# Sorting sample scores by merge steps, an earlier selection and a fifth slot for query slices in a fused decoder layer

## The reference, cut to what matters

```
z = rms_norm(x) @ w_in                      # u, q, k, v, iq, ik, iw
score = sum_h relu(iq_h . ik) * iw_h        # one score per query and key
keys  = top_k(score, k)                     # k = 64 of 256 (prompt), 256 of 1028 (sample)
yb    = softmax(q . k / sqrt(128)) over those keys @ v ;  ya = pooling mixer(u)
x1    = x + concat(ya, yb) @ w_o
q2    = rms_norm(x1) @ w_pq ;  s = q2 . sub_keys     # 16 slices of 128 columns
16 best pairs per head -> 128 experts per token
y     = x1 + sum_e g_e * gelu(h . expert_u[e]) * expert_v[e]
```

## Time and profile before

| what | us |
|---|---|
| three runs | 981.14, 981.31, 981.70 (median 981.31) |
| the profiled execution, its own time | 981.55 |
| its span, first to last instruction | 980.1 |
| PE busy | 958.2 (98% of the span) |
| DVE busy | 777.5 (79%) |
| ACT busy | 558.6 (57%) |
| POOL busy | 438.6 (45%) |

### The profile page before, as it was taken

One profiled execution on the slowest core, in us unless ns is written; L12 is line 12 of the kernel. 1 busy time (PEld: TensorE's weight loads), 2 busy tenths in 40 slices (PEclk: granted clock), 3 DMA queues, 4 the chain that ended last, 5 costly groups with the idle time before them and its releaser, 6 DMA issues.

```text
span 980.1 us, 19215 instructions
## 1 busy us (share of the span) xinstructions
PE 958.2 (98%) x6440; PEld 835.3 (85%) x6440; DVE 777.5 (79%) x1805; ACT 558.6 (57%) x1092; POOL 438.6 (45%) x328
## 2 busy tenths in 40 slices
PE   5999999999999999999999999999999999999998
PEld 2347879899999999999999998888888888888887
DVE  2569987269999948999999976777888878788873
ACT  2023354454445559999999975654555555555552
POOL 4643465145788776776777770011212211131200
PEclk9999999999999999999999999999999999999999
DMA  9635748668855554444445456797888888888872
GB/s 330 149 109 160 238 139 308 209 226 316 280 176 175 180 185 150 152 161 160 150 155 165 151 173 217 257 337 283 300 300 305 299 279 296 303 304 303 291 263 94
DMA packets 75424, 221.24 MB, mean 226 GB/s; under 512 B 11301, under 2 KB 23725, under 8 KB 74964
## 3 DMA queue, kind: packets, MB, share of 16 engines
q1 hardware_dynamic: 60812, 179.12, 53.7%
q0 software_dynamic: 12800, 40.36, 13.3%
q10 hardware_dynamic: 1744, 0.92, 0.4%
HBM read 217.41 MB, written 3.14 MB: 225 GB/s over the span
## 4 chain that ended last, share of the span: by engine, by line
PE 86%; DVE 4%; DMA 4%; ACTq 2%; ACT 2%; issue 2%; SPq 0%; DVEq 0%
PE psum L1123 33%; PE psum L1059 22%; PE psum L1060 12%; PE psum L1071 3%; PE psum L1055 3%; PE psum L603 3%; PE psum L872 2%; ACTq L402 1%; PE psum L873 1%; DMA w_raw<-expert_v 1%; DMA rows_in<-expert_u,eidx 1%; PE psum L581 1%; DMA w_raw<-expert_ut 1%; DVE work L1825 1%; PE psum L887 1%
## 5 line engine op out<-in xcount | busy, mean ns | idle before, releaser
L1630 POOL TENSOR_TENSOR w_lo<-w_raw,w_hi 128x1024 fp32r<-128x1024 f32 x116 | 279.1, 2410 | 124.1 <-ACT w_hi L1170 123.9
L1059 PE MATMUL psum<-h_split,w_hi 128*128 128x256 f32 x1792 | 327.0, 284 | 1.3 <-issue 1.3
L1060 PE MATMUL psum<-h_split,w_lo 128*128 128x256 f32 x1024 | 289.4, 283 | 0.0
L1059 PEld LDWEIGHTS psum<-h_split,w_hi 128*128 128x128 f32 x1792 | 279.2, 192 | 2.6 <-issue 1.4
L1170 ACT ACTIVATE w_hi<-w_raw 128x1024 fp32r<-128x1024 f32 x214 | 224.9, 1051 | 39.4 <-DMA w_raw<-expert_ut 27.6
L1060 PEld LDWEIGHTS psum<-h_split,w_lo 128*128 128x128 f32 x1024 | 196.1, 191 | 0.0
L2145 DVE TENSOR_TENSOR w_lo<-w_raw,w_hi 128x1024 fp32r<-128x1024 f32 x98 | 120.5, 1229 | 54.7 <-ACT w_hi L1170 54.4
L1123 PE MATMUL psum<-w_hi,ag_hi 128*128 128x512 f32 x512 | 158.2, 390 | 0.4 <-DVE ag_lo L2152 0.4
L1123 PE MATMUL psum<-w_hi,ag_lo 128*128 128x512 f32 x512 | 158.0, 389 | 0.0
L1170 ACT ACTIVATE ag_hi<-store 128x256 fp32r<-128x256 f32 x128 | 53.2, 417 | 152.5 <-PE psum L1123 152.4
L1123 PEld LDWEIGHTS psum<-w_hi,ag_hi 128*128 128x128 f32 x512 | 95.8, 188 | 20.6 <-ACT w_hi L1170 0.8
(11 more groups left out here) (347 smaller groups left out, 1485.0 us busy)
## 6 DMA issues: line engine op xcount, KB each, us to landing
w_raw<-expert_ut SPq DMA_DIRECT2D x128, 512.0 KB
w_raw<-expert_v SPq DMA_DIRECT2D x86, 512.0 KB
raw_more<-expert_v SPq DMA_DIRECT2D x42, 512.0 KB, 4.8
w_slice<-w_pq_cols SPq DMA_DIRECT2D x32, 512.0 KB, 5.3
w_most<-w_in_blocks SPq DMA_DIRECT2D x8, 699.0 KB, 11.3
w_slice<-w_o_half SPq DMA_DIRECT2D x8, 512.0 KB, 4.7
v_cache<-cache_v POOLq DMA_DIRECT2D x64, 64.0 KB, 3.7
w_o_sb<-w_o_half SPq DMA_DIRECT2D x8, 512.0 KB, 6.1
```

The costliest lines, as they stand in the source:

```text
L1059: pe.matmul(out, w_hi[:, s, c, :], h_split[:, c, a], start=(c == 0 and a == 0), stop=False)
L1060: mm = pe.matmul(out, w_lo[:, s, c, :], h_split[:, c, 0], start=False, stop=(c == KC - 1), skip_group_check=wide)
L1630: pool.tensor_tensor(w_lo[:, s], w_raw[:, s], w_hi[:, s].bitcast(F32), ALU.subtract).then_inc(S["w_lo_ready"], 1)
```

## The change

1. The 32 rounds become 36 merge steps (`sort`), each a maximum and a minimum of 128 x 128 elements over rows of 256, spread 11, 10, 5, 4, 4 and 2 over the same places; a step with d = 0 reads its second operand backwards. `insert` puts the 257th score in.
2. `join`, the eight `order` steps and `cut` all come ahead of `add_wo(0)`, `tally` and `admit` between `add_wo(0)` and `add_wo(3)`.
3. A fifth place `w_slice_x` (where `probT` lies later) for slices 4 and 9; SP loads slices 0, 4, 1, 2, 3 first, later ones as their place comes free (`before(r)`), and w_o_sb beside slices 7 to 14 instead of 6 to 13.
4. `low_q(1)` and `low_q(2)` move from POOL to DVE, `low_q(0)` ahead of `join_sq(4)` on POOL, and POOL's `v_cache` groups follow without a break. `high_q(2)` moves up on ACT, and `copy_q(r)` stands ahead of `high_q` where it stood behind it. `high_q(11)` now stands ahead of `rs_copy(1)`.

The diff, with context and assertions cut and the new `w_slice_x` and `q_lo_x` (both at `cur[0] - NPG * P`) left out:

```diff
@@ -331,12 +333,12 @@
...
     S = Named(nc, ctx)
-    w_slice_in = [ctx.enter_context(nc.semaphore(f"w_slice_in{i}")) for i in range(SLICES)]
+    w_slice_in = [ctx.enter_context(nc.semaphore(f"w_slice_in{i}")) for i in range(SLICES + 1)]
     row_in = [ctx.enter_context(nc.semaphore(f"row_in{i}")) for i in range(2)]
...
-    Q_FIRST = 3
+    Q_FIRST = 1
@@ -345,9 +347,28 @@
...
+    R_SLOT = (0, 1, 2, 3, 4, 0, 1, 2, 3, 4, 0, 1, 2, 3, 0, 1)
+    assert len(R_SLOT) == RSLOTS and KC == 2 * SLICES
+    def r_turn(r):
+        return (2 if R_SLOT[r] < SLICES else 0) + R_SLOT[:r + 1].count(R_SLOT[r])
+    def s_turn(i, j):
+        return 2 + R_SLOT.count(j) + i + 1
+    def before(r):
+        return max([x for x in range(r) if R_SLOT[x] == R_SLOT[r]], default=-1)
+    def q_raw(r):
+        return w_slice[:, R_SLOT[r]] if R_SLOT[r] < SLICES else w_slice_x[:]
...
-        return q_lo[:, (KC + r) % SLICES]
+        return q_lo[:, R_SLOT[r]] if R_SLOT[r] < SLICES else q_lo_x[:]
@@ -459,21 +480,30 @@
...
-            Q_PQ, Q_SAMPLE = KC, KC + RSLOTS
...
-                old = q - SLICES
-                if old >= Q_SAMPLE:
-                    sp.wait_ge(S["rq_s_psum"], (old - Q_SAMPLE) // 4 + 1)
-                elif old >= Q_PQ:
-                    sp.wait_ge(S["rq_psum"], old - Q_PQ + 1)
-                elif old >= 4:
-                    sp.wait_ge(S["wo_psum"], 2 * (old - 4) + 2)
-                elif old >= 0:
-                    sp.wait_ge(S["wo_half"], old + 1)
-                src = w_o_half[q] if q < Q_PQ else w_pq_cols[(q - Q_PQ) % RSLOTS]
-                sp.dma_start(w_slice[:, q % SLICES], src).then_inc(w_slice_in[q % SLICES], 16)
+                if q >= SLICES:
+                    sp.wait_ge(S["wo_half"], q - SLICES + 1)
+                sp.dma_start(w_slice[:, q % SLICES], w_o_half[q]).then_inc(w_slice_in[q % SLICES], 16)
+            def load_q(r):
+                if r < SLICES:
+                    sp.wait_ge(S["wo_psum"], 2 * r + 2)
+                elif before(r) < 0:
+                    sp.wait_ge(S["yb_psum"], 2)
+                else:
+                    sp.wait_ge(S["rq_psum"], before(r) + 1)
+                sp.dma_start(q_raw(r), w_pq_cols[r]).then_inc(w_slice_in[R_SLOT[r]], 16)
+            def load_sample(i):
+                for j in range(SLICES):
+                    if i:
+                        sp.wait_ge(S["rq_s_psum"], i)
+                    else:
+                        sp.wait_ge(S["rq_psum"], max(r for r in range(RSLOTS) if R_SLOT[r] == j) + 1)
+                    sp.dma_start(w_slice[:, j], w_pq_cols[SLICES * i + j]).then_inc(w_slice_in[j], 16)
@@ -491,8 +521,10 @@
...
             k_loads(32, K_SP - 32)
-            for q in range(4, 12):
+            for q in range(4, KC):
                 load_slice(q)
+            for r in (0, 4, 1, 2, 3):
+                load_q(r)
             sp.wait_ge(S["zp_copied"], 8)
@@ -505,14 +537,14 @@
...
                              ).then_inc(S["rows_out"], 16)
-            for q in range(12, 14):
-                load_slice(q)
+            for r in (5, 6):
+                load_q(r)
             sp.wait_ge(S["log_g_done"], 2)
             for i in range(8):
-                load_slice(14 + i)
+                load_q(7 + i)
                 sp.dma_start(w_o_sb[:, i].rearrange("p a k j -> p (a k) j"), w_o_half[i]).then_inc(S["w_o_in"], 16)
-            for q in range(22, Q_SAMPLE):
-                load_slice(q)
+            for r in range(15, RSLOTS):
+                load_q(r)
@@ -531,15 +563,12 @@
...
                 load_u(s, s)
-            for q in range(Q_SAMPLE, Q_SAMPLE + SLICES):
-                load_slice(q)
+            load_sample(0)
             for n in range(FRONT):
...
                 if n % 4 == 1 and n < 12:
-                    q = Q_SAMPLE + SLICES * (n // 4 + 1)
-                    for i in range(SLICES):
-                        load_slice(q + i)
+                    load_sample(n // 4 + 1)
                 if n == 8:
@@ -998,7 +1027,7 @@
...
                 for j in range(4):
-                    slice_in(KC + RSLOTS + 4 * i + j)
+                    pe.wait_ge(w_slice_in[j], 16 * s_turn(i, j))
                 if i:
@@ -1290,10 +1319,10 @@
...
-                act.wait_ge(w_slice_in[(KC + r) % SLICES], 16 * ((KC + r) // SLICES + 1))
+                act.wait_ge(w_slice_in[R_SLOT[r]], 16 * r_turn(r))
                 if 3 <= r < 13:
                     act.wait_ge(S["rq_psum"], r - 1 if r >= 11 else r - 2)
-                copy(q_high(r), w_slice[:, (KC + r) % SLICES]).then_inc(S["q_hi_ready"], 1)
+                copy(q_high(r), q_raw(r)).then_inc(S["q_hi_ready"], 1)
@@ -1301,6 +1330,7 @@
...
+            high_q(2)
             act.wait_ge(S["rstd_half"], 2)
@@ -1341,27 +1371,24 @@
...
                 copy(h_split[:, c, 0, :], h2[:, c, 0:SEQ]).then_inc(S["h_hi_p"], 1)
-            high_q(2)
             copy_log(0)
             copy_log(1)
-            for r in range(3, 7):
+            for r in range(3, 8):
+                copy_q(r - 3)
                 high_q(r)
-                copy_q(r - 3)
-            high_q(7)
-            copy_q(4)
             act.wait_ge(S["rows_out"], 16 * (9 + 1 + DB))
             rs_copy(act, copy, 0)
+            copy_q(5)
             high_q(8)
-            copy_q(5)
             sample_exp(0)
+            copy_q(6)
             high_q(9)
-            copy_q(6)
+            copy_q(7)
             high_q(10)
-            copy_q(7)
             sample_exp(1)
             copy_q(8)
+            high_q(11)
             rs_copy(act, copy, 1)
-            high_q(11)
             copy_q(9)
@@ -1618,12 +1645,9 @@
...
             join_sq(2)
+            low_q(0)
             join_sq(4)
-            low_q(0)
-            low_q(1)
-            v_loads(V_FIRST + 4, 4)
-            low_q(2)
-            v_loads(V_FIRST + 8, DB * NPG - V_FIRST - 8)
+            v_loads(V_FIRST + 4, DB * NPG - V_FIRST - 4)
@@ -1814,16 +1838,26 @@
...
-            def rounds(n):
-                for _ in range(n):
-                    r = done[0]
-                    left = score4[:, :] if r == 0 else work4[:, :]
-                    best = sorted4[:, 8 * r:8 * r + 8]
-                    settle(dve.max(best, left))
-                    if r < ROUNDS - 1:
-                        settle(dve.match_replace(work4[:, :], best, left, TAKEN))
+            lists = (sorted4, work4)
+            HALVES = [(1 << m, d) for m in range(STAGES) for d in [0] + [1 << e for e in range(m - 1, -1, -1)]]
+            def sort(n):
+                for half, d in HALVES[done[0]:done[0] + n]:
+                    old = score4 if done[0] == 0 else lists[(done[0] + 1) % 2]
+                    a, b = (x[:, 0:QK].rearrange("p (n h k) -> p n h k", h=2, k=d or half)
+                            for x in (old, lists[done[0] % 2]))
+                    one, two = a[:, :, 0], a[:, :, 1] if d or half == 1 else a[:, :, 1, ::-1]
+                    dve.tensor_tensor(b[:, :, 0], one, two, ALU.max)
+                    settle(dve.tensor_tensor(b[:, :, 1], one, two, ALU.min))
                     done[0] += 1
+            def insert(_):
+                new = score4[:, QK:QW]
+                dve.tensor_tensor(sorted4[:, 0:1], work4[:, 0:1], new, ALU.max)
+                settle(dve.scalar_tensor_tensor(sorted4[:, 1:QK], work4[:, 0:QK - 1], new, work4[:, 1:QK],
+                                                ALU.min, ALU.max))
@@ -1880,31 +1914,39 @@
...
+            def low_q(r):
+                dve.wait_ge(S["q_hi_ready"], r + 1)
+                dve.tensor_tensor(q_low(r), q_raw(r), q_high(r).bitcast(F32), ALU.subtract
+                                  ).then_inc(S["q_lo_dve"], 1)
             done = [0]
-            STAGES = 8
-            assert QK == 1 << STAGES and ROUNDS * 8 == KSEL_S == QK
-            rounds(6)
+            assert QK == 1 << STAGES and KSEL_S == QK and len(HALVES) % 2 == 0
+            sort(11)
             rope_qk(2)
-            rounds(5)
+            sort(10)
             select_p(0)
-            rounds(3)
+            sort(5)
             select_p(1)
             norm_p(0)
-            rounds(2)
+            sort(4)
             max_p(1)
-            rounds(2)
+            sort(4)
             norm_p(1)
-            rounds(ROUNDS - done[0])
+            sort(len(HALVES) - done[0])
+            insert(0)
+            join(0)
+            for stage in range(STAGES):
+                order(stage)
+            cut(0)
             add_wo(0)
-            join(0)
-            for i in range(1, 5):
+            tally(0)
+            add_wo(1)
+            add_wo(2)
+            admit(0)
+            for i in range(3, KC):
                 add_wo(i)
-                order(2 * i - 2)
-                order(2 * i - 1)
-            add_wo(5)
-            cut(0)
-            add_wo(6)
-            add_wo(7)
+            low_q(1)
             norm2_p(0)
@@ -1912,16 +1954,7 @@
...
-            def low_q(r):
```

(14 more changed lines are left out.)

## The result

Median 984.62 us over 18 runs (981.28 to 987.14) against 981.17 for the kernel before on the same chip (18 runs, 979.04 to 983.36): ratio 1.0037, 95% interval 1.0027 to 1.0047, which is 2.6 to 4.6 us **slower**. Run again beside other kernels, the changed kernel gave 1.0025 (1.0007 to 1.0043). The forecast was 981.8, with 978.8 to 984.0 as its range: the median is just outside it, and a slowdown was held to be less likely (0.24) than no change (0.57). One run of the kernel before, among those beside d1 to d4, took 5427 us and enters no ratio.

The account below looks back on a forecast made before the run. The prediction took PE, busy 98% of the span, as the bound, with about 4.8 us of idle to win. Terms 2.1 - 1.5 - 2.8 + 2.2 = 0.0 (+1.25 with DVE first) gave 981.6 or 982.8; forecast 981.8, range 978.8 to 984.0.

Parts of the forecast that it names:

- The map of the waits: Where PE's waits would go or arise: `q_ring` waits gone, new ones at the second tile's transposes and an `rs`.
- the first `rs` behind the sample copy: At `rs(8)`, PE would idle 2.2 us because `rs_copy(1)` stands behind `high_q(11)`, which waits for `rq(9)`.
- the samples' slices: Three loads go out together at 209 and arrive at 215.2, before PE wants them at 215.96: no cost.
- The sign that failed: At the output sums' end, PE's sum of squares would be done some 1.5 us after the last chunk's addition.
- Sort for rounds: On DVE, 36 merge steps at 0.51 us each, 18.4 us, would replace 32 rounds of about 31.2 us.
- rival 3: In the sort, merge steps are dearer than order steps; at 0.62 us a step the time is 984.0; chance 0.12.
- The port: POOL's `diag0` and `diag1` would block DVE's sort, making PE's second-tile transposes 2.1 us late.
- rival 1: At the second tile's transposes, the port does not stop the sort: -2.1 us, 979.5 to 980.7; chance 0.14.
- The tail of the output sums: Ahead of `norm2_p`, a gain of 1.5 us if POOL's `join_sq(4)` precedes DVE's `low_q(1)`, 0.25 if DVE is first.
- The query stage: Ahead of `rs(0)`, `rs(2)` and `rs(7)`, PE's three waits for ACT's query copies would go: -2.8 us.
- 2: `rs(8)` does not wait for the copy because something else holds PE there: -2.2 us, 979.4; chance 0.08.
- 4: Smaller mishaps (samples' slices, `high_q(2)`'s landing, DVE first at the port) add up to 2: 983.6 us; chance 0.11.

Follow-up runs that it names:

- d1: The kernel of e4 run again as a control: 978.4 us, ratio 0.9970 to the kernel before.
- d4: c3 with 7 merge steps instead of 11 ahead of `rope_qk(2)`, the other four at the end: 978.79 us, ratio 0.9982 to the kernel before.
- e3: The changed kernel with `join_sq(4)` back ahead of `low_q(0)` on POOL: 980.69 us, ratio 1.0011 to the kernel before.
- e1: The changed kernel with `rs_copy(1)` put back ahead of `high_q(11)` on ACT: 980.53 us, ratio 1.0008 to the kernel before.
- e2: The changed kernel with 7 merge steps ahead of `rope_qk(2)` and 14 behind it, instead of 11 and 10: 983.06 us, ratio 1.0028 to the kernel before.
- after: The changed kernel itself, as first measured and profiled: 984.62 us, ratio 1.0037 to the kernel before.
- c1: The changed kernel run again unchanged, as a control: 984.67 us, ratio 1.0025 to the kernel before.
- c2: The changed kernel with four spare matmuls in PE's idle piece ahead of the sums' last wait: 983.35 us, ratio 1.0027 to the kernel before.
- e4: The changed kernel with the edits of e1, e2 and e3 together: 977.53 us, ratio 0.9972 to the kernel before.
- d2: e4 with 10 merge steps instead of 14 behind `rope_qk(2)`, and `low_q(1)` on POOL instead of DVE: 976.38 us, ratio 0.9952 to the kernel before.
- c3: The kernel before with only the merge sort and insertion in place of the rounds: 979.98 us, ratio 0.9988 to the kernel before.
- c4: The kernel before with only the fifth slice place and its slice order, `sr` copied first: 984.1 us, ratio 1.0027 to the kernel before.

## Why the prediction was wrong, point by point

**The map of the waits was right but for one.** There is no `q_ring` wait, a wait of 2.27 at the first `rs` behind the sample copy (forecast 2.2), a wait at the second tile's transposes, nothing for `tally` and `admit` under the chunks, nothing at the samples' slices (of the later kernels only e3 has a wait there). e1, e2 and e3 each took one wait away, e2 and e3 with a new, shorter one in its place. The sign that failed is the sum of squares: it was to be done 1.5 us after the last chunk's addition, and was done 4.2 us after it (138.12 to 142.31).

**Sort for rounds: right.** A step was to start every 0.51 us; it is 0.53, with 0.29 and 0.28 for its halves, reversed or not, and nothing like rival 3's 0.62. Here the text was right that 128 partitions cost no more than 64. The changed kernel's sort maxima, by source line (duration ns min/median/max):

```profile
L1851 DVE TENSOR_TENSOR work<-sorted x18: 283/292/294, 67.2 to 115.6; 128x128 f32<-128x128 f32 x18
L1851 DVE TENSOR_TENSOR sorted<-work x17: 284/292/1901, 67.7 to 115.0; 128x128 f32<-128x128 f32 x17
```

**The port: right in kind, 1.6 instead of 2.1.** The prediction let POOL's short cast hold VectorE for another 0.45 us. It did not: the cast ran from 74.49 to 74.83, and VectorE's next maximum started at 74.72 and took 0.29. The 1901 ns above is the step that stood under POOL's first product, and its minimum stood under the second. DVE and POOL in the changed kernel, which answer to the earlier trace rows:

```profile
70.89 1.90 DVE L1851 TENSOR_TENSOR sorted<-work 128x128 f32<-128x128 f32 x1
72.71 1.98 DVE L1852 TENSOR_TENSOR sorted<-work 128x128 f32<-128x128 f32 x1
```

```profile
70.74 1.90 POOL L1613 TENSOR_TENSOR diag<-ident,iw 128x1024 f32<-128x1024 f32 x1 [3.93 <-PE psum L632]
72.60 1.94 POOL L1615 TENSOR_TENSOR diag<-ident,iw 128x1024 f32<-128x1024 f32 x1
74.49 0.34 POOL L1617 CAST ident<-ident 128x128 bf16<-128x128 f32 x1
```

By the recorded starts POOL was first both times, by 0.15 and by 0.11 us, the second time although DVE's minimum stood right behind its maximum. The Trainium skill (SBUF — State Buffer, "Who interferes with whom") says that the order of issue decides who blocks; these starts agree, and an operation that only stood next in DVE's queue did not count as issued. That refutes rival 1.

**The tail of the output sums: the first step that failed.** "I take POOL first, by 0.1 us, which is a toss" came out the other way, by 0.17 us (DVE, then POOL):

```profile
137.70 0.42 DVE L1808 TENSOR_TENSOR xT<-xT,psum 128x256 f32<-128x256 f32 x1 [1.31 <-PE psum L849]
138.04 1.30 DVE L1920 TENSOR_TENSOR q_lo<-w_slice,q_hi_ab 128x1024 fp32r<-128x1024 f32 x1
```

```profile
135.90 2.36 POOL L1632 TENSOR_TENSOR q_lo<-w_slice,q_hi_ab 128x1024 fp32r<-128x1024 f32 x1
138.21 1.71 POOL L1641 TENSOR_TENSOR sq<-sq 128x256 f32<-128x256 f32 x1
```

In the times of before (4.72 less) DVE started at 133.32, where the prediction has 133.37, and POOL's subtraction ended at 133.54 instead of 133.3: POOL's queue was 0.24 late, more than the 0.1 in hand. It was no matter of luck either: DVE was first in all five profiles with this order (after, c1, c2, e1, e2), by 0.09 to 0.19. The text priced this: a gain of 0.25 instead of 1.5, and a sum of +1.25. A difference of that worth, taken for a toss, should have put the predicted time between the two and the edge of the range beyond the worse one.

**What the sum had no term for: the second step that failed.** Both new waits were costed at their idle time. The price of an idle piece of 2 us is more: B lengthened by 1.17 where -0.25 was due with DVE first, and c2 shows that 1.44 us of it are the clock. Behind the wait for `sr` the low clock cost another 1.6 in three of five profiled kernels. The Trainium skill (TensorE: Matmul & The Clock Gate, "HAM oscillation — how this bites in real kernels") tells of a kernel in which PE waits for data at every tile and comes back at the low clock each time, behind waits longer than the ones here; the rows here show the fall behind a single wait of 1.97 us, and it bears against this change, which turned short idle pieces into two of about 2 us. The prediction has no term for the clock.

**The query stage: more than costed.** The three waits were 2.8 us; without them and without the new one C is 71.10 to 71.22 in e1, e4, d1 and d2 instead of 75.01, 3.8 less. Where the extra 1.0 lies can be seen by the starts of `rs`, counted from the stretch's first matmul. The kernel before is behind e4 by 0.89 at the first, 1.01 at the second, 2.14 and 2.24 at the next two, by 3.69 at the eighth and 3.79 from the ninth on. So 3.5 us come at the three marked waits and 0.3 at the `rs` right behind each, where the view of waits shows nothing. The extra is no fixed price of a stop: the single wait of 2.27 costs 2.40 (73.50 against e1's 71.10). With B, where d2 is 2.45 shorter than the kernel before, 6.2 us could be had in these stretches, more than the 4.8 of idle time that the prediction called all that there is to win.

**The sum again,** with what the traces showed at full clock: +1.6 at the transposes, -0.25 in B, -3.8 and +2.4 in C, which is about nothing. To this the low clock comes, 1.44 in B and 1.6 in C in three profiles of five, if it falls nowhere else. That would make 2.3 us. But this sum compares with an execution of the kernel before in which the clock never fell, and not all its runs are like that: the mean granted clock is below 1.000 in 50 of its 97 runs beside the experiments, and in 26 of 30 runs of the changed kernel (with c1). The means, 0.9989 and 0.9978, differ by 0.0011, which is worth 1.1 us of 980 (an estimate, if all that PE loses is added to the time). That makes about 1.0 us in all where 3.6 and, in the repetition, 2.5 were measured. **So 1.5 to 2.6 us of the slowdown stay open,** and not all of it is the clock: the four runs of the changed kernel at a mean clock of 1.000 took 982.2 us on average, the 47 of the kernel before 979.8. One place to look is the profile of before itself: with 981.55 us it is a long run for its full clock, so its stretches may be longer than usual and the gain in C overstated (its `q_ring` waits are 2.8 us, those of c3 and d4, with the same places for slices, 0.7 and 2.2). No run separates this.

**Rivals.** 1 is refuted by the blocked pair, 2 by the wait at L916, 3 by the step's time. 4 named "DVE first at the port" as one of its mishaps at 0.11: it was a part of the answer (1.25 us), and the chance was too small for what the text itself called a toss.

## What to carry to other kernels

A wait may cost more than its idle time: where the profile of TensorE shows one idle piece of about 2 us in place of several smaller ones, reckon with what it can lose at half clock behind it (1.4 to 1.6 us here, though not in every execution), or put work in front of the wait. When work is moved between queues, look for what each moved instruction now stands in front of: here `high_q(11)` before a copy, a subtraction before the joined squares, and four sort steps before a selection, each of which made PE wait 1.0 to 2.3 us and took one line or two to mend. And a slice that comes earlier starts its consumers earlier, which may fall on a busy port (c4), so the order of the consumers belongs to the same change.

## What the runs showed of the hardware that I had not expected

- **The granted clock after one idle piece.** The fourteen profiles have 18 idle pieces of PE of 1.89 to 3.71 us behind the first 20 us. With 15 of them the clock was at 0.50 when PE started again or within 2 us of it; with three it stayed at 1.00 (2.27 in after and in e2, 2.12 in d4). By place: 1.89 to 1.99 at L857, fell in four of four profiles; 2.27 at the first `rs` behind the sample copy, in three of five; 1.93 to 3.38 at the start (L648, in d4 L619), in six of seven; 3.11 at L610 in e2 and 3.71 at L884 in c4, both. Behind none of the 31 pieces of 1.0 to 1.6 us did it fall.
- **Two operations at the port take turns.** POOL got in between DVE's maximum and minimum, and one operation of DVE got in between POOL's two products (starts 70.74, 70.89, 72.60, 72.71). Beside POOL's products of two SBUF tensors, held were DVE's operations of two SBUF inputs and a scaling of 128x5 (0.89 for 0.17); not held were MAX8 (0.43) and a reduction of 640 columns (0.82, d4).
- **A reversed operand costs nothing:** 0.29 and 0.28 us for the 128 columns of a step, in every step that was not beside POOL.
